# A recurrence kernel's depthwise convolution, silu and modulation partials, redistributed over the input projection and the gate stage

## The reference, cut to what matters

```python
shift1, scale1, gate1, shift2, scale2, gate2 = jnp.split(mod[:, None, :], 6, axis=-1)   # mod = silu(c) @ w_mod + b_mod
h = rmsnorm(x, p['norm1_g']) * (1 + scale1) + shift1
xa, ub, o_pre, ga, gb = jnp.split(h @ p['w_in'], IN_SPLITS, axis=-1)
...
uc = jax.nn.silu(depthwise_conv(u, p['mlstm_conv'], rows))       # 3x3 on the 16x64 latent grid, 1x3 on the prompt
q = jnp.einsum('bthd,hde->bhte', uch, p['mlstm_w_q'])
k = jnp.einsum('bthd,hde->bhte', uch, p['mlstm_w_k']) * (B_HEAD_DIM ** -0.5)
v = jnp.einsum('bthd,hde->bhte', u.reshape(...), p['mlstm_w_v'])
log_i = jnp.einsum('btc,ch->bht', uc, p['mlstm_w_i'][d]) + p['mlstm_b_i'][d][:, None]
log_f = jax.nn.log_sigmoid(jnp.einsum('btc,ch->bht', uc, p['mlstm_w_f'][d]) + p['mlstm_b_f'][d][:, None])
```

## Time and profile before

| | |
|---|---|
| median of 3 runs | 2634.09 us (2632.74 to 2639.38) |
| the profiled execution, its own time | 2633.48 us |
| its span in the profile | 2631.8 us |
| `phase_b`, first to last instruction | 77.2 to 487.0 us |
| `phase_c_prepare`, first instruction to the first of `phase_c_scan` | 492.8 to 615.4 us |
| TensorE busy over the span | 2163.7 us (82%) |
| VectorE, ScalarE, GpSimd busy | 1012.3, 646.9, 313.1 us |

### The profile page before, as it was taken

How to read it: one execution, slowest core, us unless ns; L and a number is a source line. 1 busy time by engine, 2 the same in 40 slices (tenths; PEclk the granted TensorE clock), 3 DMA queues, 4 the chain that set the end, 5 groups by cost and what they waited for, 6 DMA issues and landing times. The chain is left out here.

```text
span 2631.8 us, 55427 instructions
## 1 busy us (share of the span) xinstructions
PE 2163.7 (82%) x24137; PEld 1734.2 (66%) x24137; DVE 1012.3 (38%) x2056; ACT 646.9 (25%) x1474; POOL 313.1 (12%) x358
## 2 busy tenths in 40 slices
PE   8899999576757779789699599799999279999950
PEld 8788888536646569579489398245455268788840
DVE  1642232545776354554544544432233200100036
ACT  2301111135634323423323333110011011111111
POOL 0000000006400111111110110311100310000012
PEclk9999999778878679789699699789999589999985
DMA  5232322103222100000000000033221089999955
GB/s 225 86 123 77 147 114 89 51 1 138 74 84 74 74 3 4 32 3 4 31 4 4 31 4 6 16 108 112 91 74 56 17 328 356 358 356 356 352 190 175
DMA packets 65085, 291.34 MB, mean 111 GB/s; under 512 B 7480, under 2 KB 19824, under 8 KB 52336
## 3 DMA queue, kind: packets, MB, share of 16 engines
q1 hardware_dynamic: 47184, 211.20, 22.1%
q0 software_dynamic: 11504, 42.00, 4.6%
q10 hardware_dynamic: 6192, 35.13, 3.5%
HBM read 236.94 MB, written 51.36 MB: 110 GB/s over the span
## 5 line engine op out<-in xcount | busy, mean ns | idle before, releaser
L2353 PEld LDWEIGHTS f_pab<-f_xt,f_w 128*128 128x128 f32 x2240 | 258.1, 194 | 17.4 <-issue 17.4
L2353 PE MATMUL f_pab<-f_xt,f_w 128*128 128x128 f32 x2240 | 258.4, 277 | 0.8 <-ACT f_xt L2383 0.8
L298 PE MATMUL b_ps<-b_h_hi,b_w_lo 128*128 128x512 f32 (+1 forms) x672 | 239.9, 357 | 8.3 <-DVE b_h_lo L347 8.3
L298 PE MATMUL b_ps<-b_h_lo,b_w_hi 128*128 128x512 f32 (+1 forms) x672 | 239.1, 356 | 0.0
L298 PE MATMUL b_ps<-b_h_hi,b_w_hi 128*128 128x512 f32 (+1 forms) x672 | 238.7, 355 | 0.0
L298 PEld LDWEIGHTS b_ps<-b_h_hi,b_w_lo 128*128 128x128 f32 x672 | 128.3, 191 | 26.0 <-issue 8.5
L1704 DVE TENSOR_TENSOR q_zz<-d_two_i,q_pn 128x128 f32<-128x128 f32 x400 | 99.9, 283 | 108.7 <-PE q_pn L1572 108.0
L298 PEld LDWEIGHTS b_ps<-b_h_hi,b_w_hi 128*128 128x128 f32 x672 | 128.1, 191 | 17.6
L298 PEld LDWEIGHTS b_ps<-b_h_lo,b_w_hi 128*128 128x128 f32 x672 | 128.3, 191 | 17.2
L1945 PE MATMUL e_pp<-y,e_wp 128*128 128x512 f32 (+1 forms) x384 | 137.7, 521 | 0.0
L2368 PE MATMUL f_po<-f_w,f_act 128*128 128x512 f32 x280 | 129.0, 603 | 3.8 <-issue 1.0
(11 more groups left out here) (367 smaller groups left out, 4334.9 us busy)
## 6 DMA issues: line engine op xcount, KB each, us to landing
f_w<-in_w SPq DMA_DIRECT2D x35, 2048.0 KB, 8.9
f_w<-in_w SPq DMA_DIRECT2D x35, 1024.0 KB, 9.2
ys_scratch<-f_out ACTq DMA_DIRECT2D x35, 512.0 KB, 8.7
y<-in_w_mod ACTq DMA_DIRECT2D x8, 2048.0 KB, 8.8
w_first<-in_w_in SPq DMA_DIRECT2D x14, 1024.0 KB, 4.8
sig_scratch<-b_stage POOLq DMA_DIRECT2D x20, 640.0 KB, 3.2
c_bc<-row_scratch SPq DMA_DIRECT2D x20, 512.0 KB, 3.8
a_wmod<-in_w_mod SPq DMA_DIRECT2D x4, 2048.0 KB, 19.9
```

The source lines that it names most:

```text
L298: mm = pe.matmul(ps[j % 2][:, n, 0:width], rounded(wt[:, j // 2, k, (j % 2) * P:(j % 2 + 1) * P]), rounded(ht[:, k, first:first + width]), ...
L2353: mm = pe.matmul(pab[:, b, w, f * P:(f + 1) * P], w13[:, b, w, k, f * P:(f + 1) * P], xt[:, b, k], start=(k == 0), stop=(k == KD - 1))
```

## The change

1. The convolution moves from `phase_c_prepare` to VectorE's queue in `phase_b`. Each of four rounds convolves one channel tile, its taps one after the other on that tile.
2. `wmod` gets a buffer of its own, of 256 columns, and `partial` has 256 columns. So there are 16 parts of half the width in place of 8, two where there was one. There is still one `partial`.
3. The four silus move to ScalarE's queue in `phase_b`, after the second gate tile of the last round.
4. The weights for q, k, v and the gates are loaded at the end of `phase_b` into `w_first`, which lives on.
5. In `phase_c_prepare` the two gates are one pass with weights of 128 columns (input gate in rows 0 to 35, forget gate from row 64). k comes before q, k in token order before v in token order. ScalarE computes the log-sigmoid before it evicts q, and the two exponentials of the row factors stand behind all 20 token groups.
6. VectorE's and ScalarE's loops of `phase_b` are written out; TensorE's and GpSimd's are still loops.

```diff
+MOD_REST = 2 * (MOD_PARTS - MOD_FIRST)
...
-        wmod = c.y[:, 4:8].rearrange("p a t -> p (a t)")[:, 0:KD * 512].rearrange("p (k n) -> p k n", k=KD)
+        wmod = ctx.enter_context(nc.sbuf_tensor("b_wmod", [P, KD, 256], F32))
...
-        partial = ctx.enter_context(nc.sbuf_tensor("b_partial", [P, 2, 512], F32))
+        partial = ctx.enter_context(nc.sbuf_tensor("b_partial", [P, 2, 256], F32))
...
+            sp.wait_ge(w_split, 14)
+            sp.dma_start(c.w_qkv, io["w_qkv"].rearrange("p a h n -> p (a h n)")).then_inc(next_in, 16)
+            sp.dma_start(c.w_if, io["w_if"].rearrange("p h n -> p (h n)")).then_inc(next_in, 16)
+            sp.wait_ge(next_in, 32)
...
             def sum_part(n):
                 pe.wait_ge(mod_term, n * TERMS + TERMS)
-                for j in range(4):
+                for j in range(2):
                     for s in range(2):
...
                 if f in (3, 5, 7):
-                    sum_part((f - 3) // 2)
+                    sum_part(f - 3)
+                    sum_part(f - 2)
             with pe.Fori(0, 5) as i:
...
-                sum_part(i + 3)
+                sum_part(i * 2 + 6)
+                sum_part(i * 2 + 7)
...
                 if f % 2 == 1 and f < 7:
                     split_w(1 + f // 4, f % 4 // 2)
-                    make_part((f - 1) // 2)
+                    make_part(f - 1)
+                    make_part(f)
             split_w(2, 1)
-            with dve.Fori(0, 4) as i:
-                make_part(i + 3)
+            dve.wait_ge(copied, 8)
+            own = Own(dve, conv_done)
+            for i in range(4):
+                make_part(2 * i + 6)
+                convolve(own, i)
+                make_part(2 * i + 7)
                 for g in range(2):
                     split_w(i + 3, g)
-            make_part(7)
-            dve.wait_ge(mod_summed, MOD_PARTS - MOD_FIRST)
+            assert own.n == CONV_STEPS, own.n
+            make_part(14)
+            make_part(15)
+            dve.wait_ge(mod_summed, MOD_REST)
...
-            with act.Fori(1, 4) as i:
-                load_part(i + 3)
+            for i in range(5):
+                if i:
+                    load_part(2 * i + 6)
                 for j in range(4):
                     sigmoids(i, j)
-                    if j % 2 == 1:
+                    if j == 0:
+                        load_part(2 * i + 7)
+                    if j % 2 == 1 and i < 4:
                         high_w(i + 3, j // 2)
-            load_part(7)
-            for j in range(4):
-                sigmoids(4, j)
+                    if i == 4 and j == 1:
+                        act.wait_ge(conv_done, CONV_STEPS)
+                        for k in range(BH):
+                            act.activation(uc[:, k], uc[:, k], ACT.Silu).then_inc(uc_set, 1)
...
-            pe.wait_ge(loaded, 96)
+            wide(0, [wif[:, k] for k in range(BH)], [uc[:, k] for k in range(BH)], gates_ready)
+            for h in range(BH):
+                if h == 1:
+                    pe.wait_ge(gates_read, 2)
+                elif h >= 2:
+                    pe.wait_ge(wide_dve, h - 1)
+                wide(1 - h % 2, [w[:, 1, h]], [uc[:, h]], wide_ready)
+            for h in range(BH):
+                if h < 2:
+                    pe.wait_ge(wide_dve, 3 + h)
+                else:
+                    pe.wait_ge(wide_act, h - 1)
+                wide(1 - h % 2, [w[:, 0, h]], [uc[:, h]], wide_ready)
             for n in range(NCH):
+                tok(n, uc, 1)
+            for n in range(NCH, 2 * NCH):
                 tok(n, c.y, 2)
-            pe.wait_ge(uc_set, BH)
```

More of the change, by code:

```diff
@@ L342, in make_part, with convolve @@
                         term.then_inc(mod_term, 1)
+            def convolve(own, k):
+                for tap, (dy, dx) in enumerate([(1, 1)] + [(a, b) for a in range(3) for b in range(3) if (a, b) != (1, 1)]):
+                    wcol = c.vec[:, conv + (3 * dy + dx) * BH + k:conv + (3 * dy + dx) * BH + k + 1]
+                    u_lat = c.y[:, k, PROMPT:].rearrange("p (r w) -> p r w", w=64)
+                    o_lat = uc[:, k, PROMPT:].rearrange("p (r w) -> p r w", w=64)
+                    if tap == 0:
+                        own.did(dve.tensor_scalar(uc[:, k], c.y[:, k], wcol, None, ALU.mult))
+                        continue
+                    own.settle()
+                    r0, r1 = max(0, 1 - dy), 16 - max(0, dy - 1)
+                    x0, x1 = max(0, 1 - dx), 64 - max(0, dx - 1)
+                    o = o_lat[:, r0:r1, x0:x1]
+                    own.did(dve.scalar_tensor_tensor(
+                        o, u_lat[:, r0 + dy - 1:r1 + dy - 1, x0 + dx - 1:x1 + dx - 1], wcol, o, ALU.mult, ALU.add))
+                    if dy == 1:
+                        x0, x1 = max(0, 1 - dx), PROMPT - max(0, dx - 1)
+                        o = uc[:, k, x0:x1]
+                        own.did(dve.scalar_tensor_tensor(
+                            o, c.y[:, k, x0 + dx - 1:x1 + dx - 1], wcol, o, ALU.mult, ALU.add))
             split_w(0, 0)
@@ L379, in load_part @@
             def load_part(n):
-                if isinstance(n, int) and n == 0:
+                if n == 0:
                     act.wait_ge(h_split, 3)
@@ L413, in _ @@
                 high_w(1 + (n - 1) // 2, (n - 1) % 2)
-                load_part(n)
+                load_part(2 * n - 1)
+                load_part(2 * n)
             for j in range(2):
@@ L489, in phase_c_prepare @@
         beta_turned = sem("c_beta_turned")
-        conv = VEC["mlstm_conv"]
         block = ctx.enter_context(nc.Block())
@@ L535, in _, with wide @@
         def _(pe):
-            def wide(n, lhs, rhs, rows):
-                if n >= 2:
-                    pe.wait_ge(wide_act if n % 2 == 0 else wide_dve, (n - 2) // 2 + 1)
+            def wide(bank, lhs, rhs, done):
                 for m, (first, width) in enumerate(BLOCKS):
                     for k in range(len(lhs)):
-                        mm = pe.matmul(ps[n % 2][0:rows, m, 0:width], lhs[k], rhs[k][:, first:first + width],
+                        mm = pe.matmul(ps[bank][:, m, 0:width], lhs[k], rhs[k][:, first:first + width],
                                        start=(k == 0), stop=(k == len(lhs) - 1))
-                mm.then_inc(wide_ready, 1)
+                mm.then_inc(done, 1)
             def tok(n, src, which):
@@ L711, in phase_c_scan @@
         sem = semaphores(nc, ctx)
-        amask, expo, sd, qi, kw = (sb(f"s_{n}", [P, 2, BH, P]) for n in ("amask", "expo", "sd", "qi", "kw"))
+        amask, expo = (c.w_first[:, 4 * i:4 * i + 4].rearrange("p k n -> p (k n)").rearrange("p (b h t) -> p b h t", b=2, h=BH) for i in range(2))
+        sd, qi, kw = (sb(f"s_{n}", [P, 2, BH, P]) for n in ("sd", "qi", "kw"))
         decay = sb("s_decay", [P, 4, BH])
@@ L2510, in program @@
         c = allocate(nc, ctx, io)
-        with (nc.sbuf_tensor("cs", [P, KD, 2], F32) as c.cs, nc.sbuf_tensor("w_first", [P, KD, 256], F32) as c.w_first,
-              nc.psum_tensor("pm", [P, 4 * MOD_PARTS, 2], F32) as c.pm):
-            phase_a(c)
-            phase_b(c)
-        phase_c(c)
+        with nc.sbuf_tensor("w_first", [P, KD, 256], F32) as c.w_first:
+            flat = c.w_first[:, :, :].rearrange("p k n -> p (k n)")
+            c.w_qkv, c.w_if = flat[:, 0:3 * BH * P], flat[:, 3 * BH * P:4 * BH * P]
+            with (nc.sbuf_tensor("cs", [P, KD, 2], F32) as c.cs,
+                  nc.psum_tensor("pm", [P, 4 * MOD_PARTS, 2], F32) as c.pm):
+                phase_a(c)
+                phase_b(c)
+            phase_c(c)
         phase_d(c)
```

98 lines of the change are left out of this document (33 added, 65 removed).

## The result

| | before | after |
|---|---|---|
| median of 4 runs each, same chip | 2633.41 us | 2659.19 us (2655.83 to 2659.74) |
| the profiled execution, its own time | 2633.48 us | 2658.68 us |
| its span | 2631.8 us | 2656.9 us |

The account below looks back on a forecast made before the run. TensorE, busy 100.00 of 100 us, was taken to bound `phase_b`; `phase_c_prepare` was a chain without such a bound. `phase_b` +72.4 (59.4 + 9.8 + 3.2) and `phase_c_prepare` −60.1 gave +12.3 on 2633.48: 2645.8 us, range 2633 to 2657.

Parts of the forecast that it names:

- The mechanism and its sign: In `phase_b`, halved parts with one `partial` stop TensorE at each of 8 sums; whole kernel 12.3 us, 0.44%, slower.
- The price of a part: In `phase_b`, VectorE makes a part of 256 columns in 7.0 us, spread 6.2 to 7.2, against 11.04 at 512.
- The cheap part: Rival: terms of 256 columns overlap fully, a part takes 4.4 us and the time is 2625.0 us; chance 0.06.
- The stops: In `phase_b`, TensorE waits for a whole part at seven stops, 8.0 to 8.8 us each, together 59.4 us.
- The clock: TensorE's clock falls at each `phase_b` stop, costing 1.4 us, bounds 0.4 and 2.1; seven times, 9.8 us.
- The clock's rival: Rival: the clock does not fall, or rises before the projection begins; 12.2 us less, 2633.6 us, no change; chance 0.10.
- The end of `phase_b`: VectorE holds the barrier; next phase begins 11.6 us after the last projection instead of 8.4, 3.2 us more.
- The cover of the convolution: In `phase_b`, one channel tile per 57 us round, 13 us allowed on VectorE, is covered and costs nothing.
- The thin cover: Rival: tap waits, loads, splits and ScalarE's queue delay the second split some 5 us in four rounds; 2666 us; chance 0.04.
- `phase_c_prepare`: Gates 11.4 us, v groups end at 48.4, exponential 51.0, scan starts at 62.5 instead of 122.6: 60.1 us shorter.
- The step that failed: From first exponential's end to scan's start stays 11.6 us; the sum has no term for anything behind the scan's start.
- The prediction's own sign of being wrong: Among the signs listed as wrong: any phase behind the scan's start that changes its length.

Follow-up runs that it names:

- experiment 1: The changed kernel with two copies of the partial sums in place of one: 2576.5 us, ratio 0.9784 to the kernel before.
- experiment 2: The kernel before with only the modulation's parts halved, two per round with one buffer, convolution not moved: 2710.57 us, ratio 1.0286.
- experiment 4: The changed kernel with 31 unused TensorE matmuls between the two sums of each pair and six behind the second: 2642.66 us, ratio 1.0034.
- experiment 7: The changed kernel with the two exponentials of the row factors ahead of the ten v groups on ScalarE: 2642.8 us, ratio 1.0034.
- experiment 5: The changed kernel with VectorE's two copies of 4 columns moved behind the scan's last step: 2651.99 us, ratio 1.0061.
- 6: The changed kernel with `sd` and `kw` laid into `w_first` in place of `amask` and `expo`: 2649.84 and 2650.4 us in two executions, no ratio.

## Why the prediction was right, and where it was wrong

- **The mechanism and its sign: right.** The parts were halved under a single `partial`, so TensorE stands still for a whole part at each pair of sums. Experiment 1 takes the stops away and the change is a gain; experiment 2 makes them alone and has the same 474 us.
- **The price of a part: right.** 7.0 us was taken from the columns, 7.03 was measured. The cheap part (rival, 0.06) fell.
- **The stops: right.** 59.4 us forecast, and 59.4 left of the 73.6 when the longer matmuls are taken off. One by one they agree too: 8.2 us for each of three (8.0, 8.0 and 8.2 forecast) and 8.7 for each of four (8.8).
- **The clock: mis-sized.** The step was "About 2 us pass with the second sum or the split, and the other 2.8 run at half speed: 1.4 us lost". The clock came back 4.5 us behind the restart of the projections, not 2.8, and 6.5 us behind TensorE's first work after the pause, where the three restarts of the kernel before had given 4.8. Why it took longer stays open. That a clock of 0.50 is half speed is borne out by the two halves of the sum, 0.94 us at 1.00 and 1.86 at 0.50. It cost 2.0 us a stop, 14.2 in the place of 9.8, which is inside the bounds given (2.1 a stop); experiment 4 gave back 12.5 net of its own 1.9. The clock's rival (0.10) fell.
- **The end of `phase_b`: right.** 11.6 us, as forecast.
- **The cover of the convolution: right.** One tile 11.7 us against 13 allowed, and 33 us of idle behind it; experiment 2 has the same projection without the move, to 0.1 us. The thin cover (0.04) fell.
- **`phase_c_prepare`: right.** 61.8 against 62.5; gates 11.3 (11.4), end of v 47.9 (48.4), exponential 50.4 (51.0). Where it said that 8 us were lost to the v groups, experiment 7 won 6.6 in this stretch.
- **The step that failed: "From the first exponential's end (603.85) to the scan's start (615.44) were 11.6 us, and that stays" was right, but the sum then took everything behind the scan's start as unchanged.** The scan became 7.3 us longer. The trace of the kernel before held a hint: a copy of 4 columns that takes 2.55 us, while operations of the same width take 0.15. I had read the scan only up to its start. Nothing in it was changed but the place of two buffers (of which the section on the reference, "The change leaves them alone", says nothing), and so no term for it stood in the sum, nor in the range. The runs put two copies there that wait for GpSimd, 3.95 and 6.59 us in place of 2.55 each (5.4 us of the 7.3; the rest is no more than the 91.4 to 93.7 us by which the scan varies with short copies); experiment 5, which moves them, takes the scan back to 93.2 us and the time to 2651.99, inside the range. The prediction's own sign of being wrong, a phase behind the scan's start that changes its length, is what came.

Those two account for the miss: +7.3 for the scan and +4.4 for the clock, and with +0.8, +1.0 and −0.7 from the other stretches it is 12.8 us between the profiled execution and 2645.8. The scan's part alone took the time out of the range.

**What stays open.** Why the copies are short in some kernels and long in others. Long (3.9 and 6.6 us, past three and seven ends of GpSimd instructions): the kernel after, two partials, both fillers. Short (2.55 to 2.57, past one): the kernel before, with halved parts, with other buffers, with early exponentials. The moment alone is not it: the first copy starts 2.26 us behind GpSimd's L913 in the kernel after and 2.23 with two partials (both long), 2.24 in the kernel before, 2.25 and 2.23 in experiments 7 and 6 (all short). Nor is the speed of GpSimd: its L902 takes 1.31 us beside the first copy of the kernel after, and 1.27 with two partials, where the copy is as long. The first copy ended 0.02 to 0.03 us behind the end of a GpSimd instruction in the kernels before and after and in experiments 1, 6 and 7, but not behind the first such end in all of them, and what chooses the one was not settled.

## What to carry to other kernels

In the kernel before, the buffer that VectorE and TensorE hand to each other once per round cost TensorE no wait, since its maker worked in the middle of the round. With the work cut in two pieces the second piece met a consumer that stood still, for up to 7.3 us each time, and a second buffer was worth 83 us (experiment 1): where work is cut like this, ask first whether the buffer is doubled. Price such a stop at the whole of the piece, 7.03 us here, plus what TensorE loses at the lower clock behind it, 2.0 us a stop here. And look in the part of the kernel that does not change for instructions that take many times as long as others of their size, as the copies of 4 columns did in the kernel before (2.55 us beside 0.15): these were waits that are recorded as work, and a change elsewhere made them longer, 3.95 and 6.59 us.

## What the runs showed of the hardware

- A copy of 4 columns within SBUF on VectorE took 2.55 to 6.59 us while GpSimd worked without gaps, and 0.13 to 0.16 us behind the scan, where GpSimd stood idle for 13.20 us; the same data as a reduction took 0.16 us beside the busy GpSimd, and 0.85 as an operation with two sources in SBUF. So the wait stands in the trace as the copy's duration.
- With 27 filling matmuls a pause of 1.17 us was left and the clock still read 0.50 behind five of seven stops; with 31 and 6 more, and a pause of at most 0.3 us, it stayed at 1.00 in all seven.
- A term of 256 columns costs 0.456 us within a part (6.38 by 14) and one of 512 columns 0.72, so half the width saves 37% of the time.
